# First modulation quarter in two blocks of 256 columns, x ahead of the weights, context loaded and transposed later

## The reference

```
mod_l = split(silu(c)     @ w_mod + b_mod, 6)     # shift, scale, gate; shift, scale, gate
mod_c = split(silu(c_ctx) @ w_mod + b_mod, 6)
n_l = rmsnorm(x,   g) * (1 + mod_l[1]) + mod_l[0]
n_c = rmsnorm(ctx, g) * (1 + mod_c[1]) + mod_c[0]
z_l = n_l @ w_in                    # 3584 columns: q 1024, k 256, v 256, gMLP u 512 and v 512, conv a 512 and g 512
z_c = n_c @ w_in[:, q_end:v_end]    # context: keys and values only
```

## Time and profile before

| | before |
|---|---|
| median of three executions | 1454.49 us |
| profiled execution, span | 1455.7 us |
| PE busy | 1305.8 us, 90% |
| DVE busy | 431.7 us, 30% |
| ACT busy | 206.0 us, 14% |
| POOL busy | 74.7 us, 5% |
| DMA moved, mean rate | 559.55 MB, 384 GB/s |

### The profile page before, as it was taken

The page is one execution under the profiler, slowest core; times in us unless marked ns, Lnnn a source line. Parts: engine busy times, 40 slices in busy tenths (PEclk is TensorE's granted clock), DMA queues, the critical chain, the costliest instruction groups (busy, mean ns, idle before and its releaser), DMA issues.

```text
span 1455.7 us, 20523 instructions
## 1 busy us (share of the span) xinstructions
PE 1305.8 (90%) x8712; PEld 627.4 (43%) x8713; DVE 431.7 (30%) x827; ACT 206.0 (14%) x481; POOL 74.7 (5%) x138
## 2 busy tenths in 40 slices
PE   3999999999999998999999999997977887878866
PEld 1656544555454565432632543442432442343223
DVE  3122597777656140201111111021110111111112
ACT  3000101244101042200210110110110110011001
POOL 0012100121132000000000000000000000000000
PEclk9899999999999899999999999999999999999988
DMA  9899868766899789999999999999999999999996
GB/s 393 342 420 407 327 257 332 285 229 246 330 359 349 278 356 427 426 428 414 427 426 421 418 425 429 400 428 427 430 427 429 429 428 429 428 430 428 429 427 260
DMA packets 57018, 559.55 MB, mean 384 GB/s; under 512 B 6640, under 2 KB 6768, under 8 KB 19952
## 3 DMA queue, kind: packets, MB, share of 16 engines
q1 hardware_dynamic: 42048, 502.24, 82.6%
q0 software_dynamic: 14320, 52.01, 9.7%
q10 hardware_dynamic: 576, 4.19, 0.7%
HBM read 556.33 MB, written 2.10 MB: 384 GB/s over the span
## 4 chain that ended last, share of the span: by engine, by line
PE 59%; DMA 33%; DVE 4%; issue 2%; ACT 1%; DVEq 0%; POOL 0%; SPq 0%; ACTq 0%; POOLq 0%
DMA ring<-w_up_dram 13%; DMA ring<-w_gate_dram 12%; PE ps L874 10%; PE ps L879 8%; PE ps L597 8%; PE ps L841 5%; PE ps L898 5%; DMA ring<-w_half_dram 3%; PE ps L700 3%; PE ps L904 3%; PE ps L591 3%; PE ps L602 2%; DMA ring<-w_in_dram 2%; DMA big<-w_up_dram 2%; PE ps L510 1%
## 5 line engine op out<-in xcount | busy, mean ns | idle before, releaser
L1585 DVE TENSOR_TENSOR big<-ps,big 128x1024 f32<-128x1024 f32 x60 | 70.7, 1220 | 309.0 <-PE ps L827 163.0
L879 PE MATMUL ps<-ring,big 128*64 128x512 f32 x560 | 131.2, 601 | 21.8 <-DMA ring<-w_up_dram 10.6
L597 PE MATMUL ps<-ring,big 128*128 128x512 f32 x320 | 145.3, 596 | 2.0 <-DMA ring<-w_in_dram 2.0
L1230 DVE SCALAR_TENSOR_TENSOR once<-ring,silu_c,once 128x1024 f32<-128x1024 f32 x96 | 123.2, 1283 | 66.3 <-DMA ring<-w_half_dram 61.2
L841 PEld LDWEIGHTS ps<-probs,big 128*128 128x128 f32 x1024 | 120.2, 193 | 44.2 <-issue 37.5
L841 PE MATMUL ps<-probs,big 128*128 128x96 f32 x1024 | 130.6, 281 | 1.9 <-DVE probs L1589 1.9
L874 PE MATMUL ps<-ring,early 128*32 128x256 f32 x1408 | 92.3, 412 | 34.0 <-DMA ring<-w_up_dram 17.6
L700 PE MATMUL ps<-ring,big 128*128 128x512 f32 x256 | 116.0, 611 | 0.0
L597 PEld LDWEIGHTS ps<-ring,big 128*128 128x128 f32 x320 | 58.7, 190 | 71.2 <-issue 66.4
L879 PEld LDWEIGHTS ps<-ring,big 128*64 128x64 f32 x560 | 35.8, 136 | 103.0 <-issue 65.6
L874 PEld LDWEIGHTS ps<-ring,early 128*32 128x32 f32 x1408 | 45.0, 116 | 81.0 <-issue 27.3
(11 more groups left out here) (308 smaller groups left out, 1133.9 us busy)
## 6 DMA issues: line engine op xcount, KB each, us to landing
ring<-w_down_dram SPq DMA_DIRECT2D x48, 2048.0 KB, 22.9
ring<-w_up_dram SPq DMA_DIRECT2D x46, 2048.0 KB, 22.8
ring<-w_gate_dram SPq DMA_DIRECT2D x33, 2048.0 KB, 21.7
ring<-w_half_dram POOLq DMA_DIRECT2D x96, 512.0 KB, 6.6
big<-w_up_dram SPq DMA_DIRECT2D x18, 2048.0 KB, 21.5
ring<-w_mix_dram SPq DMA_DIRECT2D x32, 1024.0 KB, 11.6
late<-w_down_dram SPq DMA_DIRECT2D x16, 2048.0 KB, 23.1
big<-w_gate_dram SPq DMA_DIRECT2D x15, 2048.0 KB, 24.5
```

The source lines that it names most:

```text
L597: mm = pe.matmul(ps[:, b + t, :], nT[:, k, t * P:(t + 1) * P], w, start=(k == 0), stop=(k == KT - 1))
L879: mm = pe.matmul(out_b[1][REST * f:REST * (f + 1), :], rows[1][:, k, :], w[:, kk, f * N:(f + 1) * N], start=(k == 0), stop=(k == KT - 1))
L1230: stt(total, half_slots[:, m % HALF_SLOTS, :], silu_c[:, m % KT, 0:1], total, ALU.mult, ALU.add) \
L1585: tt(y, Yb[:, 2 * h:2 * h + 2, :].rearrange("p a n -> p (a n)"), y, ALU.add).then_inc(summed, 1)
```

## The change

- The first block of 512 modulation columns becomes two blocks of 256: `BLOCKS` lists (first k-tile, number of k-tiles) of five blocks. Their weights come from a new array `w_mix0`, in which a chunk holds eight k-tiles of 256 columns; a part of a block then takes two chunks. The w_in pieces of k-tiles 0 to 3 for a, g and q0 are loaded as two halves each, each in a slot of its own.
- x is issued by SP, ahead of all weight chunks. Its transposes are split into steps of four k-tiles and mixed with the first `mod` and `ext` steps; group a starts when the transposes of banks 0 and 1 are saved.
- ctx is issued by ACT behind block 2's rows, squared and scaled at block 3, and transposed in eight steps `ctxT` (banks M and T) between the products of the last block; ACT saves them all.
- POOL waits until ctx is scaled before it issues the remaining tables and parameters and the first four half rows; it modulates the context only as `ctxT` steps are saved, with two half rows behind each group of four k-tiles. The large constant table is issued behind the last `mod` chunk.
- DVE sums 3 half rows behind the last block, builds `rope` there, and then sums 10.

```diff
+BLOCKS = ((0, 2), (2, 2), (4, 4), (8, 4), (12, 4))
+NB = len(BLOCKS)
...
+    seq = [("mod", 0, 0, 0), ("mod", 0, 0, 1)] + [("tok", 0, q) for q in range(4)]
+    seq += [("mod", 0, 1, 0), ("ext", 0, 0), ("mod", 0, 1, 1), ("tok", 1, 0), ("ext", 0, 1)]
+    seq += [("tok", 1, q) for q in range(1, 4)]
+    context = [("ctxT", i) for i in range(8)]
+    for j, (k0, nk) in enumerate(BLOCKS):
+        following = [("mod", j + 1, p, c) for p in range(2) for c in range(BLOCKS[j + 1][1])] if j + 1 < NB else []
+        half = len(following) // 2
+        win = [[("win", g, k0 + i) for i in range(nk)] for g in (A_, G_, Q0_)]
+        if j + 1 < NB:
+            seq += win[0] + following[:half]
+            seq += win[1][0:nk // 2] + [("ext", j + 1, 0)] + win[1][nk // 2:]
+            seq += following[half:] + win[2][0:1] + [("ext", j + 1, 1)] + win[2][1:]
+        else:
+            steps = [s for w in win for s in w]
+            for n, step in enumerate(steps):
+                seq.append(step)
+                if n in (1, 3, 4, 5, 6, 7, 8, 9):
+                    seq.append(context.pop(0))
...
+            for t in range(TT):
+                sp.dma_start(tokens[:, t, :], x[t * P:(t + 1) * P, :]).then_inc(x_in[t], 16)
...
-                if n == PRE_SLOTS - 1:
-                    sp.dma_start(const[:, P:], consts[:, P:CONST_COLS]).then_inc(table_in, 16)
+                if n == NUMBER["mod", NB - 1, 1, 3]:
+                    sp.dma_start(const[:, FIRST_CONSTS:], consts[:, FIRST_CONSTS:CONST_COLS]).then_inc(table_in, 16)
...
-            pool.wait_ge(ctx_in, 16 * TT)
+            pool.wait_ge(scaled, 2 * TT)
...
+            for m in range(HALF_SLOTS):
+                load_rows(m)
+            for q in range(4):
+                pool.wait_ge(scale_done, q + 2)
+                pool.wait_ge(ctxT_saved, 2 * q + 2)
+                for k in range(4 * q, 4 * q + 4):
                     pool.tensor_scalar(nT[:, k, SEQ:2 * SEQ], nT[:, k, SEQ:2 * SEQ], scale_mix[:, k, 1:2],
                                        modcol[:, 0, k, 1:2], ALU.mult, ALU.add).then_inc(nC_ready, 1)
...
+                for m in range(HALF_SLOTS + 2 * q, HALF_SLOTS + 2 * q + 2):
+                    load_rows(m)
...
+                    if j < 2:
+
+                        for i in range(8):
+                            at = 32 * (i % 4)
+                            mm = pe.matmul(bank[at:at + 32, 0:256], silu_c[:, 8 * c + i, :],
+                                           slot(n)[:, i * 256:(i + 1) * 256], start=(c == 0 and i < 4),
+                                           stop=(c == 1 and i >= 4))
...
+                elif kind == "ctxT":
+                    i = step[1]
+                    q, t = i // 2, i % 2
+                    if i == 0:
+                        pe.wait_ge(modcol_saved, 2 * NB)
+                        pe.wait_ge(scaled, 2 * TT)
+                    if i > 1:
+                        pe.wait_ge(ctxT_saved, i - 1)
+                    for i in range(4):
+                        k = 4 * q + i
+                        mm = pe.transpose((T if t else M)[:, i * P:(i + 1) * P], early[:, t, k * P:(k + 1) * P], ident)
+                    mm.then_inc(ctxT_done, 1)
...
+            for j in range(1, NB):
                 for p in range(2):
...
+                    save_rows(j, p)
+                if j == 2:
+                    for t in range(TT):
+                        act.dma_start(tokens[:, TT + t, :], ctx[t * P:(t + 1) * P, :]).then_inc(ctx_in, 16)
+                elif j == 3:
+                    act.wait_ge(ctx_in, 16 * TT)
+                    for t in range(TT):
+                        squares_of(TT + t)
+            save_ctxT(0)
+            save_ctxT(1)
             act.wait_ge(slot_free, used(A_))
             copy(bufA[:], ps[:, 0:2, :]).then_inc(a_saved, 1)
+            for i in range(2, 6):
+                save_ctxT(i)
...
+                if j == 0:
+                    save_tokT(1, 2)
+                elif j == 3:
+                    scale_tokens(TT)
...
+            sum_rows(3)
...
-            sum_rows(6)
+            sum_rows(10)
```

More of the change, by code:

```diff
@@ L117, with first_row @@
 SCHEDULE = make_schedule()
-CHUNK_STEPS = [s for s in SCHEDULE if s[0] in ("mod", "wout", "gate") or (s[0] == "win" and s[2] % 4 == 0)]
+def first_row(g, k):
+    return k // 2 * 2 if g in (A_, G_, Q0_) and k < 4 else k // 4 * 4
+CHUNK_STEPS = [s for s in SCHEDULE if s[0] in ("mod", "wout", "gate") or (s[0] == "win" and s[2] == first_row(*s[1:]))]
 NPRE = len(CHUNK_STEPS)
@@ L180, with build @@
 CONST_COLS = CONST_AT["cos"][0]
-def build(nc, x, ctx, params, consts, b_half, b_gate, w_mix, w_half, w_gmod, w_in, w_out, w_gate, w_up, w_down, out):
+FIRST_CONSTS = CONST_AT["before"][0]
+def build(nc, x, ctx, params, consts, b_half, b_gate, w_mix0, w_mix, w_half, w_gmod, w_in, w_out, w_gate, w_up, w_down, out):
     with ExitStack() as stack:
@@ L522, in _ @@
                 elif kind == "tok":
[L523 to L530, removed]
-                        mm.then_inc(tokT_done, 1)
+                    t, q = step[1:]
+                    if q == 0:
+                        pe.wait_ge(scaled, t + 1)
+                    if t:
+                        pe.wait_ge(tokT_act if q % 2 else tokT_dve, q // 2 + 1)
+                    for i in range(4):
+                        k = 4 * q + i
+                        mm = pe.transpose(Z[q][:, i * P:(i + 1) * P], early[:, t, k * P:(k + 1) * P], ident)
+                    mm.then_inc(tokT_done, 1)
+                elif kind == "ctxT":
[6 more added lines that the diff above has]
+                        pe.wait_ge(ctxT_saved, i - 1)
+                    for i in range(4):
+                        k = 4 * q + i
+                        mm = pe.transpose((T if t else M)[:, i * P:(i + 1) * P], early[:, t, k * P:(k + 1) * P], ident)
+                    mm.then_inc(ctxT_done, 1)
                 elif kind == "half":
@@ L961, in _ @@
             copy = nc.scalar.copy
-            for t in range(2 * TT):
-                act.dma_start(tokens[:, t, :], (x if t < TT else ctx)[(t % TT) * P:(t % TT + 1) * P, :]) \
-                    .then_inc(tok_in if t < TT else ctx_in, 16)
             act.wait_ge(zeroed, 1)
@@ L984, in save_rows, with squares_of @@
[L984 to L992 removed]
+            def squares_of(t):
+                nowhere = ring[:, PRE_SLOTS + t % TT, :] if t >= TT else nT_all[:, t * D:(t + 1) * D]
+                act.activation(nowhere, tokens[:, t, :], ACT.Square,
+                               accum_out=ss[:, t:t + 1]).then_inc(sumsq_done, 1)
@@ L1247, in _, with scale_tokens @@
-            save_tokT(3)
+            def scale_tokens(t0):
+                dve.wait_ge(sumsq_done, t0 + TT)
+                link(ts(stat[:, 0:2], ss[:, t0:t0 + 2], 1.0 / D, EPS, ALU.mult, ALU.add))
+                rsqrt(rs_tok[:, t0:t0 + 2], stat[:, 0:2], stat[:, 4:6])
+                if t0:
+                    dve.wait_ge(tokT_done, 4 * TT)
+                for t in range(t0, t0 + TT):
+                    ts(early[:, t % 2, :], tokens[:, t, :], rs_tok[:, t:t + 1], None, ALU.mult).then_inc(scaled, 1)
@@ L1279, in head_norm @@
+            link(ts(neg_sink[:], sink, -1.0, None, ALU.mult))
+            for i in range(2):
+                for t in range(TT):
+                    g = qk_gain[:, i, :]
+                    cs, sn = (k_(n)[:, t * HD:(t + 1) * HD] for n in ("cos", "sin"))
+                    link(tt(rope[:, 2 * i, t, :], cs, g, ALU.mult))
+                    for a in (0, 64):
+                        link(tt(rope[:, 2 * i + 1, t, a:a + 64], sn[:, a:a + 64], g[:, 64 - a:128 - a], ALU.mult))
             def head_norm(idx):
@@ L1708 @@
         "b_gate": np.repeat(b_mod[5 * D:6 * D].reshape(4, N), P // 4, 0),
-        "w_mix": tiles(w_mod, [p * D + b * N for b in range(4) for p in range(2)]),
+        "w_mix0": np.stack([w_mod[:, p * D + j * 256:p * D + (j + 1) * 256] for j in range(2) for p in range(2)])
+            .reshape(4, 2, 8, P, 256).transpose(0, 1, 3, 2, 4).reshape(8, P, CH),
+        "w_mix": tiles(w_mod, [p * D + b * N for b in range(1, 4) for p in range(2)]),
         "w_half": w_mod[:, 2 * D:5 * D].reshape(KT, P, 6, HALF).transpose(2, 0, 1, 3).reshape(6 * KT, P, HALF),
```

211 lines of the change are left out of this document (93 added, 118 removed).

## The result

The changed kernel takes 1468.57 us (median of 6, 1463.95 to 1472.5) against 1454.89 (median of 6): ratio 1.0077 [1.0051, 1.0102], some 11 us (7 to 15). I had forecast 1456.0 with a range of 1448.5 to 1462.

The account below looks back on a forecast made before the run. DMA was taken to bound the start, PE the stretch from q0 of block 2. The later of PE (-0.6) and DVE (0 to +2.5), taken as +1.5, gave span 1457.2, carried to median 1456.0; range 1448.5 to 1462.

Parts of the forecast that it names:

- Bytes and start: DMA queue up to q0 of block 2: 51.7 MB at 0.42 MB/us; group a near 27 us, q0 at 131.
- the 4 us of holes: DMA ahead of q0 of block 2: small idle holes while ring slots are full, 4 us in sum, bounds 0 and 7.
- My check of the sum against 136.98: Same byte sum for the kernel before: 135.5 us against 136.98 traced for q0 of block 2, perhaps 1 to 2 early.
- The 1.2 us from the last byte to the landing: DMA completion: 1.2 us added to the byte sum for the chunk of q0 of block 2.
- PE tail: PE from q0 of block 2 (7.96 us) to q0's end: 28.6 us plus context transposes, ending at 163.5 to 165.0.
- rival C: Early PE: idle at 10 to 27 us keeps the clock at 1.2 GHz; +5 us, 1459.5, chance 0.08.
- The context transposes: PE tail: 32 transposes moved in from ahead of the first a, 3.9 us, bounds 3.5 and 5.1.
- DVE: DVE before head 0: late half rows start the q statistics at 177.5, 8.6 us later; head 0 0 to 2 later.
- The slack of 8.92 us: DVE's idle times from the q statistics to head 0, 8.92 us, expected to absorb the 8.6 us delay.
- rival B: DVE: half rows 4 to 12 late, q statistics after 178, each us beyond one us; +4, 1459.5, chance 0.22.
- A shift at the hand-over goes 1:1 into the end: From DVE's maximum for head 0 (264.20 us) on, the chain was to move unchanged, passing any shift to the end.
- differs by more than 1 us: Sign of being wrong: the rest behind head 0's maximum differing from before by more than 1 us.

Follow-up runs that it names:

- e7: Changed kernel plus 32 small PE products, half rows 4 to 6 issued earlier, tables and parameters loaded only once the last block is scaled; ratio 0.9972 to before.
- e2: Changed kernel plus 32 small PE products ahead of the first step, 257 more PE instructions than before; 1458.33 us, ratio 1.0026 to before.
- e4: Changed kernel with 32 filler products of 256 columns in PE's waits ahead of q0 of block 2; 1462.17 us, ratio 1.0064 to before.
- e3: Changed kernel plus 32 small PE products, with POOL issuing half rows 4 to 6 ahead of its first wait for context transposes; 1457.43 us, ratio 1.0026 to before.
- e6: Kernel before plus 64 small PE products (256 instructions) behind the wait for silu(c); ratio 1.0004 to before.
- e1: Kernel before plus 32 small PE products (128 instructions) ahead of the first step; 1463.6 us, ratio 1.0069 to before.
- e11: Kernel before plus 48 small PE products (192 instructions) ahead of everything; ratio 1.0022 to before.

## Why the prediction was wrong

- *Bytes and start: the start of q0 right, by terms that were wrong and made up for each other.* Group a came at 24.4 (forecast 27) and q0 of block 2 at 132.20 (131; range 129 to 134). But the 4 us of holes in that sum aren't there: the DMA share was 1.00 from 28 to 50 us. Without them the sum gives 126.8. In their place the engines moved less in a busy microsecond (403 GB/s from 28 to 50 us, before 420) and some 0.8 MB more than counted had moved 1.2 us ahead of the start (52.5 MB by 131, at a mean of 401 GB/s). Whether the half-size pieces or the shorter rows of `w_mix0` made them slower was not tried. My check of the sum against 136.98 was none: in before PE didn't wait for that chunk, as my own landmarks say. The 1.2 us from the last byte to the landing was an estimate for which I showed no row. That ctx, tables and parameters still stand ahead of the chunk that sets the pace was the point: e7 moved them behind it and gained.
- *PE tail: the term for q0 of block 2 was mis-sized.* I carried its 7.96 us over from before; it took 12.27, since PE had idled in front of it and the clock was at 0.50. I had this mechanism as rival C, but at 10 to 27 us, where the clock stood at 1.00. The idle time moved to where PE now waits for the DMA, right ahead of the tail. The context transposes took 3.5 us, as taken (3.9). The end of q0 came at 168.69, not 163.5 to 165.
- *DVE: mechanism right, size off.* The q statistics were forecast at 177.5 and came at 179.08. The slack of 8.92 us was then gone, as forecast; but rows 17 to 20 waited 1.51, 4.50 and 2.48 us, and head 0 came 4.8 late instead of 0 to 2. These rows waited 8.5 us in sum; before, the same four waited 4.7 (2.01, 0.30 and 2.36). The sum that I should have made is 10.2 later, less 8.9 of slack, and 3.8 more of waits: 5.1, against 4.8 measured. That the number is near rival B's price (+4) is luck: by B's own rule, one us for each beyond 178, 179.08 would have given 1.1. In e2 and e4 these rows waited 8.6 and 9.7 us too, and come one each 3.8 us, so it is no single collision; what sets that spacing is open.
- *"A shift at the hand-over goes 1:1 into the end": the step that failed.* It needs a rest of equal length, and I had priced the 256-column products only in time (0.88 against 0.89 us a chunk), not in instructions. The rest grew by 7.8 us (926.8 to 934.6). In all kernels whose loop stands at the old place modulo 256 (0, 256 or 257 more) it is 925.1 to 926.9, whatever head 0 does. The part from head 0 to the experts isn't as rigid: in e2 head 0 is 2.0 later and the span 2.1 longer, but in e3 and e6 head 0 is 2.4 and 2.3 later and the experts start 0.35 and 0.5 earlier than in before. Of the 9.9 us between the two profiles, 7.8 are the place of the loop and 2.1 the new order. Timed, the new order alone has a ratio of 1.0026 [1.0002, 1.0051], 1458.33 us (e2): inside the predicted range, and the place alone 1.0069 [1.004, 1.0098] (e1).
- *The chances.* No rival had a mechanism behind the hand-over; the "differs by more than 1 us" in my list of what would show me wrong is what happened: from head 0's maximum to the end it was 1191.5 us before and 1196.6 after. Two signs of being right failed as well, both by the tail: from the start of q0 of block 2 to the end of q0 36.5 us (31 to 33.5), and DVE idle 8.5 us for rows 17 to 20 alone (under 3).

## What to carry to other kernels

Count instructions as well as time: when an edit adds or removes PE instructions ahead of a loop whose code is fetched anew in each pass (look at the queue for instructions), a pass can take 1 to 5% longer with nothing else changed (e1), so compare variants at the same place modulo 256, and look for "issue" waits that cut a run of like instructions. A queue that is in order makes every byte ahead of the pacing chunk count, whoever needs it; moving 1.4 MB behind that chunk gained. And when PE is made to wait less early, look at where it now waits: here the clock was at its lower level behind that wait, and 8 us of products took 9.8 to 12.3.

## What the runs showed of the hardware

- 9 instruction packets of 16.7 KB a pass come over the DMA engines. With 128 or 129 instructions more ahead of the loop PE stops for 1.6 to 2.4 us a pass, one such packet starting as it does (inferred: a late block of PE's code). An "issue" piece of 4.4 to 5.1 us stands at the entry into the loop in all kernels but e11, where it is 9.98.
- Adding 0, 64, 128, 192 and 256 small PE instructions gave a rest of 926.8, 925.8, 937.5, 928.6 and 926.1 us.
- The granted clock came down to 0.50 after PE was busy 1.18 of 5 us (120 to 125 us in after), and how long it stays there differs between kernels that are alike in that stretch (after to 140 us, e2 to about 135).
